# Normalising by feature tile: the input rows are turned once, the conditioning weights come in wider rows

## The chip, the cores and the metric

One core of a Trainium2 chip runs one launch of the kernel. The metric is the device time of that launch in microseconds. Engines are called by their functions: TensorE (PE; its weight loads are PEld), VectorE (DVE), ScalarE (ACT), GpSimd (POOL), and SyncE (SP), whose queue issues nearly all the DMAs.

## The reference

One inference step of a decoder layer for 1024 prompt tokens and 8 x 4 sample tokens, width 1024, all in float32. The first lines are those that matter here:

```python
mod = jax.nn.silu(c) @ w_ada + b_ada                      # one row per sequence (9 of them), 6 * 1024 columns
sh1, sc1, g1, sh2, sc2, g2 = split(mod, 6)
h = rmsnorm(x, norm_mix_w) * (1.0 + sc1) + sh1            # x * rsqrt(mean(x*x) + EPS) * w
z = h @ w_in + b_in                                       # 8 slices of 1024 columns
```

z feeds an HGRN2 recurrence with 8 heads of 128 and a gated depthwise convolution over 31 tokens; the two are gated, joined, multiplied by w_out and added to x; then come a second norm, a SwiGLU feed-forward part of width 2816 and a last norm. The six outputs are y for both groups and both groups' recurrent and convolution states.

## The kernel before

**Layout.** Everything is kept turned: features on the 128 partitions, the 1056 tokens (1024 prompt, 32 sample) along the free axis, 8 feature tiles (NJ). A float32 product is made of three: each operand is split in a high part and a low part (the rest), and hi*hi, hi*lo and lo*hi are summed. So for each block of weights (128 columns, 512 KB) ScalarE makes w_hi, VectorE or GpSimd makes w_lo = w_raw - w_hi (the helper low), and TensorE multiplies them with h_hi and h_lo in three groups of 352 tokens.

**The head of the program,** which the change rewrites, runs once before all of that. SP's queue (from L504) loads the conditioning vectors, four tiles of 128 tokens of x in four row buffers, 13 small loads of vectors, the conditioning weights of feature tile 0 (load_mod, L516: shift and scale, 512 KB each, in rows of 128 columns, that is 512 bytes), the other five tiles of x as the row buffers come free, the first two blocks of w_in, and the conditioning weights of tiles 1 to 7, for which there are three buffers (WADA). Each load into a used buffer waits for its readers.

For each tile t of tokens, ScalarE squares the row with a running sum (L1836), GpSimd makes the root's reciprocal rs9 (L2130, L2132), VectorE multiplies the row by it into xn (L1263). TensorE turns both x and xn, 8 transposes of 128x128 each, into PSUM (turn, L790). ScalarE copies x out of PSUM to xt (L1829), which is kept for the residual; VectorE copies the normed one to xh (L1256). In between VectorE and ScalarE do the small work on the lower bounds (lower_bounds, L1242). ScalarE and GpSimd split the two first blocks of w_in (L1813, L2107).

Then, for each feature tile j, TensorE makes the conditioning products in four groups of 32 rows (conditioning, L814: 32 products), ScalarE copies them out (acols, L1849), TensorE sums the groups (fold_groups, L827), and VectorE adds the bias (L1276), makes am = (1 + sc1) * w (L1283), then the modulated tile twice over: ScalarE writes its high part h_hi (L1851 for the prompt, L1853 for the samples) and VectorE the whole in float32 (L1287, with L1290 and L1292 for the 32 sample tokens), from which it takes h_hi to get h_lo (L1294). As soon as a feature tile is there, first_tiles (L835) multiplies it with both of the first two blocks of w_in: 9 matmuls for a block, 18 for a feature tile. Conditioning for tile kt + 2 goes ahead of tile kt's products, and its fold between the two blocks:

```python
for kt in range(NJ):
    if kt + 2 < NJ:
        conditioning(kt + 2)
    ...
    pe.wait_ge(h_ready, kt + 1)
    for b in range(2):
        ... 9 matmuls ...
        if b == 0 and kt + 2 < NJ:
            fold_groups(kt + 2)
```

After the last feature tile, the first block's PSUM banks are read, and the steady part begins: z_tile (L894) for each head, the convolution taps and the recurrence on VectorE beside it, and later the merge and the feed-forward products. It is the same in both kernels. SP issues there in program order: w_in blocks 2 and 3, the old convolution rows, then the store of xt (4.2 MB in two DMAs) which the residual reads much later.

Every wait is a semaphore written out by hand. The order of one engine is its program order; Steps.settle makes an engine wait for its own last instruction. GpSimd starts making masks (L2144) after the last h_ready.

## Time and profile before

| | |
|---|---|
| median of 3 runs | 1974.66 us (1973.8 to 1977.93) |
| the profiled execution's own time | 1975.14 us |
| its span in the profile | 1973.4 us |
| mean granted TensorE clock | 0.994 |
| TensorE busy | 1935.4 us, 16182 matmuls |
| VectorE, ScalarE, GpSimd busy | 1316.6, 655.9, 232.5 us |
| DMA | 237.45 MB, mean 120 GB/s |

A row of the view by line names the line, engine, operation, tiles, shapes and count, then busy time and mean ns of one, then the idle time before them. A row of the timeline or of the chain begins with start and duration in us. A busy engine overlaps its own instructions at the ends, so the distance between the starts of two that follow each other is a little less than a duration. TensorE's clock is given as a share of 2.4 GHz; 0.50 is its lower level of 1.2 GHz.

### The profile page before, as it was taken

What the parts mean: (1) busy time and instruction counts of PE and PEld (TensorE: products, weight loads), DVE (VectorE), ACT (ScalarE), POOL (GpSimd) and SP (SyncE); (2) the same over time, 40 slices, a digit from 0 to 9 for tenths busy, and PEclk for the clock granted to TensorE, in tenths of its full rate; (3) what the DMA queues carried; (4) which work ended last, traced back from release to release, by engine and by line L of the source; (5) the groups of instructions that cost most, each with busy time, mean ns of one, the idle gap of its engine ahead of it and who ended that gap; (6) DMA issues with size and microseconds to landing.
All of it is one profiled execution on the core that took longest, in us unless ns stands there. A gap on an engine that the chain in (4) does not pass through costs nothing.

```text
span 1973.4 us, 39636 instructions
## 1 busy us (share of the span) xinstructions
PE 1935.4 (98%) x16182; PEld 1876.1 (95%) x16182; DVE 1316.6 (67%) x1800; ACT 655.9 (33%) x1066; POOL 232.5 (12%) x256
## 2 busy tenths in 40 slices
PE   7999999999999999998999999999999999999998
PEld 6999999999999999988989999999999999999998
DVE  6697979786878788897775665554445544465543
ACT  6212313131413222233544433333343333433332
POOL 2300000000000000021132554700000000000000
PEclk8999999999999999999999999999999999999999
DMA  8723041413232222222366644444444544444443
GB/s 254 229 61 87 24 112 45 112 45 92 66 90 67 70 77 79 78 75 93 107 216 210 187 135 139 132 138 140 136 137 143 154 136 136 135 147 148 138 133 110
DMA packets 417245, 237.45 MB, mean 120 GB/s; under 512 B 16375, under 2 KB 411287, under 8 KB 417072
## 3 DMA queue, kind: packets, MB, share of 16 engines
q1 hardware_dynamic: 416672, 234.48, 40.6%
q8 instruction: 118, 1.93, 0.4%
q10 hardware_dynamic: 416, 0.72, 0.1%
q14 instruction: 39, 0.32, 0.0%
HBM read 211.91 MB, written 24.11 MB: 120 GB/s over the span
## 4 chain that ended last, share of the span: by engine, by line
PE 83%; DVE 10%; ACT 3%; issue 2%; DMA 1%; DVEq 0%; POOL 0%; ACTq 0%; SPq 0%
PE Z L887 45%; PE Z L905 27%; DVE yb L1453 4%; DVE w_lo L1305 2%; PE R L980 1%; PE Z L852 1%; PE R L924 1%; ACT w_hi L1813 1%; PE R L1006 1%; PE R L930 1%; PE R L1013 1%; PE R L1015 1%; PE R L987 1%; DVE S L1420 1%; DMA w_raw<-in_w_out_dram 1%
## 5 line engine op out<-in xcount | busy, mean ns | idle before, releaser
L1813 ACT ACTIVATE w_hi<-w_raw 128x1024 fp32r<-128x1024 f32 (+1 forms) x316 | 329.4, 1043 | 932.3 <-PE Z L887 469.7
L1305 DVE TENSOR_TENSOR w_lo<-w_raw,w_hi 128x1024 fp32r<-128x1024 f32 (+1 forms) x305 | 386.0, 1266 | 369.1 <-ACT w_hi L1813 361.4
L905 PE MATMUL Z<-h_hi,w_hi 128*128 128x352 f32 x1488 | 499.7, 336 | 2.8 <-issue 1.7
L905 PE MATMUL Z<-h_hi,w_lo 128*128 128x352 f32 x1488 | 478.4, 321 | 0.0
L905 PE MATMUL Z<-h_lo,w_hi 128*128 128x352 f32 x1488 | 477.8, 321 | 0.0
L1453 DVE SCALAR_TENSOR_TENSOR yb<-up,vec,yb 128x1024 f32 (+1 forms) x240 | 327.2, 1363 | 28.8 <-DVE yb L1453 3.7
L887 PE MATMUL Z<-h_hi,w_hi 128*128 128x352 f32 x1056 | 342.1, 324 | 0.0
L887 PE MATMUL Z<-h_hi,w_lo 128*128 128x352 f32 x1056 | 339.2, 321 | 0.0
L887 PE MATMUL Z<-h_lo,w_hi 128*128 128x352 f32 x1056 | 338.6, 321 | 0.0
L905 PEld LDWEIGHTS Z<-h_hi,w_hi 128*128 128x128 f32 x1488 | 279.5, 188 | 20.2 <-issue 16.7
L905 PEld LDWEIGHTS Z<-h_lo,w_hi 128*128 128x128 f32 x1488 | 280.3, 188 | 0.5 <-issue 0.5
L905 PEld LDWEIGHTS Z<-h_hi,w_lo 128*128 128x128 f32 x1488 | 279.3, 188 | 0.0
L887 PEld LDWEIGHTS Z<-h_lo,w_hi 128*128 128x128 f32 x1056 | 198.7, 188 | 0.0
L887 PEld LDWEIGHTS Z<-h_hi,w_lo 128*128 128x128 f32 x1056 | 198.4, 188 | 0.0
L887 PEld LDWEIGHTS Z<-h_hi,w_hi 128*128 128x128 f32 x1056 | 198.1, 188 | 0.0
L887 PE MATMUL Z<-act_hi,w_hi 128*128 128x352 f32 x528 | 170.8, 323 | 0.0
L887 PE MATMUL Z<-act_hi,w_lo 128*128 128x352 f32 x528 | 169.6, 321 | 0.0
L887 PE MATMUL Z<-act_lo,w_hi 128*128 128x352 f32 x528 | 169.3, 321 | 0.0
L887 PEld LDWEIGHTS Z<-act_hi,w_lo 128*128 128x128 f32 x528 | 99.4, 188 | 0.0
L887 PEld LDWEIGHTS Z<-act_lo,w_hi 128*128 128x128 f32 x528 | 99.2, 188 | 0.0
L887 PEld LDWEIGHTS Z<-act_hi,w_hi 128*128 128x128 f32 x528 | 99.1, 188 | 0.0
L2190 POOL TENSOR_TENSOR gate<-ta,tb 128x1056 f32<-128x1056 f32 x8 | 21.2, 2645 | 626.0 <-DVE O L1439 480.8
(303 smaller groups left out, 2408.8 us busy)
## 6 DMA issues: line engine op xcount, KB each, us to landing
w_raw<-in_w_ffn_in_dram SPq DMA_DIRECT2D x132, 512.0 KB, 3.8
w_raw<-in_w_in_dram SPq DMA_DIRECT2D x64, 512.0 KB, 5.0
w_raw<-in_w_out_dram SPq DMA_DIRECT2D x48, 512.0 KB, 4.2
w_raw<-in_w_ffn_out_dram SPq DMA_DIRECT2D x48, 512.0 KB, 4.0
aw<-in_w_ada_dram SPq DMA_DIRECT2D x32, 512.0 KB, 4.0
w_raw<-in_w_ffn_out_dram SPq DMA_DIRECT2D x24, 384.0 KB, 3.4
ada_w<-in_w_ada_dram SPq DMA_DIRECT2D x16, 512.0 KB, 6.2
mbuf<-merged_scratch SPq DMA_DIRECT2D x32, 176.0 KB, 4.3
```

Of the source, the lines that this page charges most:

```text
L852: last = mm(Z[b][:, g, 0:GW], w[:, kt, :], x[:, kt, g * GW:(g + 1) * GW], start=kt == 0 and m == 0, stop=kt == NJ - 1 and m == 2)
L887: last = mm(out, w[:, kt, :], x(kt, g), start=first and kt == 0 and m == 0, stop=last_block and kt == n - 1 and m == 2)
L905: last = mm(out, w[:, kt, :], x[:, kt, cols], start=kt == 0 and m == 0, stop=kt == NJ - 1 and m == 2)
L924: return transpose(out, in_, ident[0:m, 0:m])
L930: last = mm(bank[group:group + 32, ADA_COL:ADA_COL + P], ct[:, kt, :], aw[:, kt, :], start=kt < 4, stop=kt >= 4)
L980: last = mm(bank[p:p + BAND, c * w:(c + 1) * w], k[:, t:t + BAND], halves(qd[:, t:t + BAND], 1 << lv, 1), start=True, stop=True)
L987: last = mm(bank[p:p + b, c * b:(c + 1) * b], k[:, t:t + b], qd[:, t + b:t + 2 * b], start=True, stop=True)
L1006: last = mm(bank[:, c * P:(c + 1) * P], ktok[:, cc, :], vtok[:, cc, :], start=True, stop=True)
L1305: st.tell(V.tensor_tensor(w_lo[b.par][:, 0:n, :], w_raw[b.par][:, 0:n, :], w_hi[b.par][:, 0:n, :].bitcast(F32), ALU.subtract), w_split, b. ...
L1453: ins = V.scalar_tensor_tensor(yp, xp, w, yp, ALU.mult, ALU.add)
L1813: A(w_hi[b.par][:, 0:n, :], w_raw[b.par][:, 0:n, :], ACT.Copy).then_inc(w_hi_ready, 1)
L2190: st.tell(Q.tensor_tensor(gate[:, :], ta[:, :], tb[:, :], ALU.mult), gate_ready, h.v)
```

## The change

The normed rows xn and their turning are gone. x alone is turned, and VectorE copies it out of PSUM, where ScalarE did. The reciprocal roots, one per token, are spread over all partitions by nine small products (root_row: rs9's column times the identity) and copied to rsrow, a row of 1056 per partition. For each feature tile VectorE multiplies xt by am and by rsrow in one operation with two SBUF inputs (scale_prompt), ScalarE adds the shift as it writes h_hi, and VectorE adds the shift and takes h_hi away in a second such operation (prompt_low). In VectorE's order the scaling of tile j stands ahead of the low part of tile j - 1. The 32 sample tokens move to GpSimd (samples: four small operations for each feature tile) with a semaphore of their own, hs_ready. The fold goes after the second of the three product groups of the first block. The lower bounds move in among the feature tiles.

All nine tiles of x have buffers of their own, in the memory of h_hi and h_lo, so no load of x waits. The conditioning weights come for two feature tiles at a time, in rows of 256 columns (1 KB): four pairs of 2 x 1 MB, two buffers. The first pair goes behind all of x; the third waits for conditioning 1, the fourth for conditioning 3. On GpSimd the first samples stand between the low parts of the two first blocks. The diff, cut:

```diff
-XN = 8
-WADA = 3
+WADA = 2
-XBUF = 4
...
-    xn, xh = at("xn", [P, XN, D], F32, A1), at("xh", [P, NJ, T], F32, A2)
+    xrow = at("xrow", [P, NC + 1, D], F32, A1)
...
+    ada_w = [e(f"ada_w{i}", [P, 2, 8, 2 * P]) for i in range(WADA)]
+    rsrow = e("rsrow", [P, T])
+    xs, hs = e("xs", [P, NJ, TS]), e("hs", [P, NJ, TS])
...
             def load_x(t):
-                if t >= XBUF:
-                    sp.wait_ge(x_squared, t - XBUF + 1)
-                    sp.wait_ge(xn_scaled, t - XBUF + 1)
-                    sp.wait_ge(x_turned, 2 * (t - XBUF + 1))
...
+            def load_mod(pair):
+                if pair >= WADA:
+                    sp.wait_ge(ada_done, 2 * (pair - WADA + 1))
                 for sec in (SH1, SC1):
+                    col = sec * D + 2 * pair * P
+                    sp.dma_start(ada_w[pair % WADA][:, sec, :, :], wada_v[:, :, col:col + 2 * P]) \
+                        .then_inc(adaw_loaded[pair % WADA], 16)
...
-            load_mod(0)
-            for t in range(XBUF, NC + 1):
+            for t in range(4, NC + 1):
                 load_x(t)
...
+            load_mod(0)
             for b in range(2):
                 load_first(b)
-            for j in range(1, NJ):
-                load_mod(j)
+            for pair in range(1, NJ // 2):
+                load_mod(pair)
...
+            def root_row(t):
+                m = tokens(t)
+                pe.wait_ge(rms_ready, t + 1)
+                wait(pe, row_copied, t - 2)
+                mm(row_bank(t), rs9[0:m, t:t + 1].to_broadcast([m, P]), ident[0:m, 0:m], start=True, stop=True) \
+                    .then_inc(row_made, 1)
...
             for t in range(NC + 1):
-                pe.wait_ge(x_loaded[t % XBUF], 16 * (t // XBUF + 1))
-                turn(t, xrow[t % XBUF], 0, x_turned, x_evac)
-                if t:
-                    turn_normed(t - 1)
+                turn_tokens(t)
+                if t >= 2:
+                    root_row(t - 2)
...
                     pe.wait_ge(h_ready, kt + 1)
+                    pe.wait_ge(hs_ready, kt + 1)
                     for b in range(2):
                         for m, (w, x) in enumerate(((w_hi[b], h_hi), (w_hi[b], h_lo), (w_lo[b], h_hi))):
...
+                            if b == 0 and m == 1 and kt + 2 < NJ:
+                                fold_groups(kt + 2)
...
-                        if b == 0 and kt + 2 < NJ:
-                            fold_groups(kt + 2)
...
-                st.do(V.tensor_scalar(buf[:, 0:TP], xh[:, j, 0:TP], am[:, j, 0:1], mod[:, SH1 * NJ + j, 0:1],
-                                      ALU.mult, ALU.add))
...
+            def scale_prompt(j):
                 st.settle()
+                st.tell(V.scalar_tensor_tensor(hbuf[j % 3][:, 0:TP], xt[:, j, 0:TP], am[:, j, 0:1], rsrow[:, 0:TP],
+                                               ALU.mult, ALU.mult), h_full, j + 1)
+            def prompt_low(j):
                 dve.wait_ge(h_hi_ready, j + 1)
+                st.tell(V.scalar_tensor_tensor(h_lo[:, j, 0:TP], hbuf[j % 3][:, 0:TP], mod[:, SH1 * NJ + j, 0:1],
+                                               h_hi[:, j, 0:TP].bitcast(F32), ALU.add, ALU.subtract), h_ready, j + 1)
+
+            condition(0)
+            condition(1)
+            scale_prompt(0)
+            for j in range(1, NJ + 1):
+                if 1 < j < NJ:
+                    condition(j)
+                if j < NJ:
+                    scale_prompt(j)
+                prompt_low(j - 1)
+                if j == 2:
+                    lower_bounds_in()
+                if j == 5:
+                    lower_bounds()
+            dve.wait_ge(hs_ready, NJ)
...
+            for j in range(2):
+                groups_out(j)
+                hi(Idx(j))
+            for j in range(NJ):
+                act.wait_ge(h_full, j + 1)
+                A(h_hi[:, j, 0:TP], hbuf[j % 3][:, 0:TP], ACT.Identity, bias=mod[:, SH1 * NJ + j, 0:1]) \
+                    .then_inc(h_hi_ready, 1)
+                if 0 < j < NJ - 1:
+                    groups_out(j + 1)
...
-            for b in range(2):
-                low(Idx(b))
+            pool.wait_ge(row_copied, NC + 1)
+            pool.wait_ge(x_evac, N_TURNS)
+            st.tell(Q.tensor_tensor(xs[:, :, :], xt[:, :, TP:T], rsrow[:, TP:T].unsqueeze(1).to_broadcast([P, NJ, TS]),
+                                    ALU.mult), xs_scaled, 1)
+            low(Idx(0))
+            def samples(j):
+                pool.wait_ge(am_ready, j + 1)
...
+                st.do(Q.tensor_tensor(seqs(xs[:, j, :]), seqs(xs[:, j, :]), per_seq(am[:, j, 1:NSEQ]), ALU.mult))
+                st.settle()
+                st.do(Q.tensor_tensor(seqs(h_hi[:, j, TP:T]), seqs(xs[:, j, :]), shift, ALU.add))
+                st.do(Q.tensor_tensor(seqs(full), seqs(xs[:, j, :]), shift, ALU.add))
+                st.settle()
+                st.tell(Q.tensor_tensor(h_lo[:, j, TP:T], full, h_hi[:, j, TP:T].bitcast(F32), ALU.subtract),
+                        hs_ready, j + 1)
+            samples(0)
+            low(Idx(1))
+            for j in range(1, NJ):
+                samples(j)
```

## Rows read from the trace of the kernel before

**Rows 1.** The page, part 1: busy us, share of the span, instructions.

```profile
PE 1935.4 (98%) x16182; PEld 1876.1 (95%) x16182; DVE 1316.6 (67%) x1800; ACT 655.9 (33%) x1066; POOL 232.5 (12%) x256
```

**Rows 2.** Stretches: us, busy of each engine (instructions), TensorE's clock, DMA share, GB/s.

```profile
0.00:31.50 31.50, 22.36 (x156) 20.49 (x156) 19.54 (x34) 23.89 (x43) 9.95 (x34) 0.95 0.87 264
31.50:40.70 9.20, 5.55 (x105) 4.52 (x105) 8.49 (x18) 3.13 (x5) 3.69 (x2) 0.73 1.02 271
...
35.80:42.60 6.80, 4.75 (x43) 4.24 (x44) 5.66 (x12) 3.35 (x6) 0.00 (x0) 0.50 0.96 251
```

**Rows 3.** The chain that ended last, 0 to 76 us: start, duration, what.

```profile
1.21 1.87 DMA crow<-in_c_sample_dram
...
38.87 1.87 PE R L823 x32
40.74 2.49 PE Z L852 x9
...
66.39 5.91 PE Z L852 x36
...
74.71 0.14 issue
```

**Rows 4.** TensorE's timeline, one feature tile.

```profile
45.05 1.08 PE L823 MATMUL R<-ada_w,ct 128*32 128x128 f32 x32
46.06 0.76 PE L852 MATMUL Z<-h_hi,w_hi 128*128 128x352 f32 x3
...
47.14 0.65 PE L852 MATMUL Z<-h_hi,w_lo 128*128 128x352 f32 x3
47.63 0.51 PE L831 MATMUL R<-fold,acols 128*128 128x9 f32 x4
...
49.62 1.08 PE L823 MATMUL R<-ada_w,ct 128*32 128x128 f32 x32
```

**Rows 5.** The view by line, each shape apart, of the first 75 us.

```profile
L1256 DVE COPY xh<-Z 128x512 f32<-128x512 f32 x16 | 10.5, 687 | 3.3 <-PE Z L797 3.2
```

**Rows 6.** Timelines of VectorE and of GpSimd, 30 to 36 us.

```profile
31.41 1.49 DVE L1244 TENSOR_TENSOR lbs<-lbs 128x8 f32<-128x8 f32 x1
...
33.17 2.04 DVE L1248 TENSOR_TENSOR lbs<-lbs 128x8 f32<-128x8 f32 x1
...
30.52 4.67 POOL L2107 TENSOR_TENSOR w_lo<-w_raw,w_hi 128x1024 fp32r<-128x1024 f32 x2 [1.42 <-ACT w_hi L1813]
```

**Rows 7.** Stretches as above, by what the DMAs moved in them.

```profile
0.00:10.00 10.00, 4.37 (x24) 4.38 (x25) 2.95 (x4) 6.68 (x10) 3.57 (x19) 1.00 0.67 234
...
4.00:8.00 4.00, 2.37 (x15) 2.38 (x16) 2.15 (x3) 2.76 (x6) 1.03 (x3) 1.00 0.98 363
...
24.00:32.00 8.00, 6.75 (x71) 5.62 (x73) 7.53 (x14) 7.39 (x16) 3.68 (x7) 1.00 1.19 298
...
64.00:70.00 6.00, 6.00 (x52) 5.80 (x42) 4.31 (x9) 3.21 (x5) 0.00 (x1) 1.00 1.03 411
```

**Rows 8.** Timelines of VectorE (two stretches) and of ScalarE.

```profile
48.17 0.36 DVE L1276 TENSOR_SCALAR mod<-R,vec 128x9 f32<-128x9 f32 x2 [1.14 <-PE R L831]
...
48.90 0.81 DVE L1287 TENSOR_SCALAR ta<-xh,am,mod 128x1024 f32<-128x1024 f32 x1
...
50.33 1.26 DVE L1294 TENSOR_TENSOR h_lo<-ta,h_hi 128x1056 fp32r<-128x1056 f32 x1 [0.30 <-ACT h_hi L1853]
...
88.97 1.28 DVE L1453 SCALAR_TENSOR_TENSOR yb<-up,vec,yb 128x1024 f32<-128x1024 f32 x1
90.17 1.22 DVE L1305 TENSOR_TENSOR w_lo<-w_raw,w_hi 128x1024 fp32r<-128x1024 f32 x1
...
32.73 0.39 ACT L1849 ACTIVATE acols<-R 128x256 f32<-128x256 f32 x1 [1.34 <-PE R L823]
```

**Rows 9.** The 32-token GpSimd operation of the second norm: ns min/median/max.

```profile
L2280 POOL TENSOR_TENSOR h2buf<-h2buf,mod x8: 241/243/402, 1244.3 to 1281.7; 128x32 f32<-128x32 f32 x8
```

**Rows 10.** A stretch as above, after the middle of the run.

```profile
1001.60:1008.50 6.90, 6.61 (x23) 5.80 (x22) 6.90 (x13) 2.05 (x3) 1.56 (x2) 0.51 0.46 157
```

More of the change, by code:

```diff
@@ L324, in program @@
     ht = e("ht", [P, NJ, NS * HIST])
-    ada_w = [e(f"ada_w{i}", [P, 2, 8, P]) for i in range(WADA)]
-    xrow = [e(f"xrow{i}", [P, D]) for i in range(XBUF)]
+    ada_w = [e(f"ada_w{i}", [P, 2, 8, 2 * P]) for i in range(WADA)]
     vrow = e("vrow", [P, 4, P])
+    rsrow = e("rsrow", [P, T])
+    xs, hs = e("xs", [P, NJ, TS]), e("hs", [P, NJ, TS])
     hbuf = (ta, tb, ysum)
@@ L788, in vectors, with turn_tokens @@
                 last.then_inc(p0_done, 1)
-            def turn(t, row, normed, done, read):
+            def turn_tokens(t):
+                pe.wait_ge(x_loaded[t], 16)
                 m = tokens(t)
                 for n in range(2 * t, 2 * t + 2):
-                    wait(pe, read, n - 2)
-                    bank = turn_bank(normed, n)
+                    wait(pe, x_evac, n - 2)
+                    bank = turn_bank(n)
                     for j in range(4):
-                        last = transpose(bank[:, j * m:(j + 1) * m], row[0:m, (4 * (n % 2) + j) * P:(4 * (n % 2) + j + 1) * P],
-                                         ident[0:m, 0:m])
-                    last.then_inc(done, 1)
-            def turn_normed(t):
-                pe.wait_ge(xn_scaled, t + 1)
-                turn(t, xn[:, t % XN, :], 1, xn_turned, xn_evac)
+                        c = (4 * (n % 2) + j) * P
+                        last = transpose(bank[:, j * m:(j + 1) * m], xrow[0:m, t, c:c + P], ident[0:m, 0:m])
+                    last.then_inc(x_turned, 1)
+            def root_row(t):
[4 more added lines that the diff above has]
+                    .then_inc(row_made, 1)
             for t in range(NC + 1):
-                pe.wait_ge(x_loaded[t % XBUF], 16 * (t // XBUF + 1))
-                turn(t, xrow[t % XBUF], 0, x_turned, x_evac)
-                if t:
-                    turn_normed(t - 1)
+                turn_tokens(t)
+                if t >= 2:
+                    root_row(t - 2)
                 if t == 2:
                     vectors()
-            turn_normed(NC)
+            for t in range(NC - 1, NC + 1):
+                root_row(t)
             def conditioning(j):
-                pe.wait_ge(adaw_loaded[j % WADA], 32 * (j // WADA + 1))
+                pair, c = j // 2, j % 2 * P
+                pe.wait_ge(adaw_loaded[pair % WADA], 32 * (pair // WADA + 1))
                 if j < 2:
@@ L823, in conditioning @@
                         last = mm(R[j % 2][group:group + 32, sec * P:(sec + 1) * P], ct[:, kt, :],
-                                  ada_w[j % WADA][:, sec, kt, :], start=kt < 4, stop=kt >= 4)
+                                  ada_w[pair % WADA][:, sec, kt, c:c + P], start=kt < 4, stop=kt >= 4)
                 last.then_inc(ada_done, 1)
@@ L1842, in _ @@
                     A(lbs[:, 1, :], lbs[:, 1, :], ACT.Exp).then_inc(lb_exp, 1)
-            turned_evac(NC)
-            for b in range(2):
-                hi(Idx(b))
-            for j in range(NJ):
-                act.wait_ge(ada_done, j + 1)
-                A(acols[:, j % 2, :, :].rearrange("p s n -> p (s n)"), R[j % 2][:, 0:2 * P], ACT.Copy).then_inc(acols_ready, 1)
-                act.wait_ge(am_ready, j + 1)
-                A(h_hi[:, j, 0:TP], xh[:, j, 0:TP], ACT.Identity, bias=mod[:, SH1 * NJ + j, 0:1], scale=am[:, j, 0:1])
-                act.wait_ge(h_full, j + 1)
-                A(h_hi[:, j, TP:T], hbuf[j % 3][:, TP:T], ACT.Copy).then_inc(h_hi_ready, 1)
             A(ms9[:, 0:1], eps[:, :], ACT.Sigmoid)
@@ L2133, in _ @@
                         rms_ready, t + 1)
-            for b in range(2):
-                low(Idx(b))
+            pool.wait_ge(row_copied, NC + 1)
[5 more added lines that the diff above has]
+                pool.wait_ge(am_ready, j + 1)
+                if j == 0:
+                    pool.wait_ge(xs_scaled, 1)
+                full, shift = hs[:, j, :], per_seq(mod[:, SH1 * NJ + j, 1:NSEQ])
+                st.do(Q.tensor_tensor(seqs(xs[:, j, :]), seqs(xs[:, j, :]), per_seq(am[:, j, 1:NSEQ]), ALU.mult))
[9 more added lines that the diff above has]
+                samples(j)
             pool.wait_ge(h_ready, NJ)
```

76 lines of the change are left out of this document (28 added, 48 removed).

## The prediction, made before the changed kernel ran

> **What bounds the kernel now.** I read the page first: TensorE is busy 1935 us of a span of 1973 us [rows 1]. Nothing in the change touches the heads, the merge or the feed-forward part, so all it can do is move the moment from which TensorE hardly stops again. The view of stretches finds it: the first 31.5 us hold 22.4 us of matmuls, the next 9.2 us only 5.6 [rows 2]. After that the chain stays on TensorE until the first block is done.
>
> The chain of the first 75 us gives the two marks of the head [rows 3]: the first product of the first feature tile starts at 40.74, and the first block's last product ends at 66.39 + 5.91 = 72.3. Behind it a block is split on ScalarE and VectorE and the steady part begins, 0.14 us after VectorE ends. All that stays, so the quantity to forecast is by how much 72.3 moves.
>
> **The head, as it is.** Between 40.7 and 72.3 TensorE is the bound: one feature tile costs 4.57 us, from conditioning at 45.05 to the next at 49.62 [rows 4]: 1.01 for 32 conditioning products, 3.56 for the two blocks with the fold between them. VectorE needs 3.42 us of the 4.57 (48.17 to 51.59 [rows 8]), and has its low part ready long before it is wanted.
>
> **What the change removes.** (1) The second turning: 72 TensorE transposes, nine scalings and 18 copies on VectorE, of 0.69 us at full size [rows 5]. In their place VectorE makes the 18 copies of x that ScalarE made, and nine row copies of a quarter of that width. 18 x 0.69, one more for the vectors and nine of a third of that, 0.23, make 15.2 us at most. TensorE turned its first tiles within the first 10 us [rows 7], so from about 8 they end near 23. They end at 31.4 now, where the lower bounds begin [rows 6]. (2) The lower bounds leave the road to the first tile. They took from 31.41 to 35.4 there, since two additions and products of eight columns lasted 1.49 and 2.04 us and both ended as a GpSimd w_lo did: two of those fill 30.52 to 35.19, 2.35 us each, and the ends are 32.90 and 35.21 [rows 6]. That is worth some 3 us at that place, but the head start meets other limits first.
>
> **The weights' arrival becomes the first of them.** The first 10 us moved 2.34 MB [rows 7], which is the first four tiles of x and the vectors. The other 2.23 MB of x are now issued at about 8.4, where the first conditioning load stood, without waiting for buffers: at the 363 GB/s that x had [rows 7], they are through at 16.1. Behind them comes the first pair, 2.10 MB in rows of 1 KB. No row has such rows; 512-byte rows moved at 298 GB/s and 4-KB rows at 411 [rows 7]. I take 350, the middle: 6.0 us, to 22.1. From the last byte to the semaphore I allow 1.0 us (between nothing and the 1.87 us for which the chain waits for the first load, 32 KB in all [rows 3]). So conditioning can begin at 23.1. The two blocks of w_in (1.05 MB at 298) follow until 25.6, the second pair until 31.6, and it is signalled at 32.6. Conditioning of tile 2 stands in TensorE's queue ahead of the first product and needs that pair. TensorE idles before it, as it did before the stretch of 0.50 clock [rows 2], where the same 32 products took 1.87 instead of 1.01 [rows 3, 4]: the first product can't start before 34.5.
>
> **The port is the second.** Conditioning 0 at 23.1, 1.01; evacuation 0.39 and 0.04 to start the next; fold 0.54 (47.63 to 48.17); conditioning 1 until 26.1; evacuation and fold until 27.1; VectorE's bias and scale 0.73 (48.17 to the scaling at 48.90), to 27.8 [rows 4, 8]. Meanwhile the first block (landed at 24.9) has its high part made on ScalarE by 25.9 (a 1024-column pass is about 1 us on it), and GpSimd's w_lo runs from 25.9 to 28.3. The new prompt operations have two SBUF inputs like the ones that stalled at 31.41, so I let them exclude GpSimd's. From 28.3, in any order: three VectorE operations of 1.28 us (two scalings and the first low part, priced by the 1.28 us of the tap product of the same shape [rows 8]), four sample operations of 0.24 [rows 9] and the second w_lo, 2.35: 7.15 us, to 35.45, and 0.14 from VectorE's end to TensorE's start [rows 3]. The first product starts at 35.6: 5.1 us earlier than 40.74.
>
> Whether VectorE also keeps GpSimd out, these rows do not isolate. The Trainium skill's page "SBUF — State Buffer" (SBUF: two separate sides) says that it does: whichever starts first has the shared ports for its whole instruction. Without that, GpSimd's small operations would cost nothing here and the first product would start 1.0 us earlier.
>
> **Then the head start is eaten.** This is the step I weigh most. The new order on VectorE is bias and scale of tile j, scaling of tile j, low part of tile j-1. The next product tile needs that low part, and it now stands behind a fold that is made in the tile before. One round: six products 1.08 (46.06 to 47.14 [rows 4]), the fold to VectorE's start 0.54, bias and scale 0.73, the scaling 1.20 (pitch of such operations back to back [rows 8]), the low part 1.28, 0.14 to TensorE: 4.97 us against TensorE's own 4.57. The old code made the same low part without another 1.28 us operation ahead of it. ScalarE's evacuation is ready about 0.7 us before the fold wants it. Six rounds, then the last three half tiles: 5.91 us for four halves now [rows 3], so 4.4. From 35.6: 29.8 + 4.4 = 69.8. A first tile at half clock adds 1.0 (its first block took 2.49 us [rows 3] where a later one took 1.57 [rows 4], 0.92). A GpSimd sample operation between VectorE's two adds 0 to 0.24 each round; I take 0.1, in all 0.6. Sum: 71.4 against 72.3, 0.9 us earlier.
>
> **Costed at nothing.** The nine root products (TensorE would wait for 23.1 anyway; if the weights came earlier, the last root, near 20.6, would show). The third load of a pair waits for conditioning 1, near 26, long before the queue reaches it; the fourth for conditioning 3, about 4.6 us after the first product, so at 40.2; it lands by 48.5, and is wanted four rounds after the first product, at 55: 6 us of cover. SP's w_in blocks, the old convolution rows and the x store stand behind it, and are not wanted before 72. ScalarE's wait for the lower bounds falls into its idle time.
>
> **Against the times.** The profiled execution took 1975.1 us for its span of 1973.4; the median is 1974.7. Taking off 0.9 gives 1974.2 and 1973.8: I forecast 1973.8 for the median. A measurement tells 0.2%, 3.9 us, from no change.
>
> **Rivals.**
> - *Faster.* The pair lands early and the clock is up: conditioning 2 ends near 33.7; VectorE and GpSimd slip past each other, first product at 33.9; the round is 4.8, between TensorE's 4.57 and my 4.97. 33.9 + 28.8 + 4.4 = 67.1, 5.2 us earlier, 1969.5. For it: 411 GB/s was seen, and TensorE worked at full clock just before its long wait [rows 2]. Against it: no row lets the low part come sooner. 26%.
> - *The wide rows bring nothing.* At 298 GB/s the first pair is signalled at 24.1 and the second at 34.7; conditioning 2 ends at 36.6, the first product starts at 36.7, the end is 72.5, 1974.9. In this the change does not do what its second half says. Also within 0.2%. For it: 298 was a steady rate with the engines always busy. Against it: the 4-KB rate is higher, so length counts. 14%.
> - *Slower.* GpSimd's four sample operations, released by the same signal as VectorE's scaling, all fall into VectorE's chain: 4 x 0.24 makes the round 5.93 instead of 5.07, six times 0.86 is 5.2 us, the end 76.6, 4.3 later, 1979.0. It decides from a round of 5.8 us. For it: the stalls at 31.41 and 33.17. Against it: only one GpSimd operation can be waiting at a time, and two of the four follow on another's end. 14%.
>
> The Trainium skill speaks for the second: "DMA: Bandwidth & Descriptors" (Specifications) puts full rate at 512 bytes and more, so doubling a 512-byte row would be worth nothing. This trace disagrees in part (298 against 411 GB/s), but between different kinds of transfer.
>
> **How the numbers follow.** The forecast has 46%, and lies within 0.2% with the second rival: same 60%, faster 26%, slower 14%. The range reaches to the faster rival's 1969.5; upward it takes the late weights (1.1 us), one more for a whole tile at half clock and a round of 5.3 (1.4 us): 1977.3, short of the slower rival. One thing outside the head can move: a stretch of half clock at 1001.6 to 1008.5 [rows 10], where 6.9 us of products lose about 3. It follows a stretch in which TensorE waited, and may fall elsewhere.
>
> **What would show it.** Right: no DVE wait of 1.5 and 2 us ahead of the first conditioning; first product near 35.6; rounds of about 5.0 with TensorE waiting for the low part's line; first steady product near 74. Wrong: rounds of 4.6 (then the gain is the head start's whole 4 to 5 us), or of 5.8; a fourth pair that TensorE waits for; DMA under 300 GB/s between 16 and 32 us.

## The result, and the profile after

The changed kernel takes 1980.7 us in the median of nine runs (1979.3 to 1982.9), the kernel before 1976.8 us in nine (1973.8 to 1977.9): a ratio of 1.0022, interval 1.0014 to 1.0030. It is slower by 4 us where a gain of 0.9 was forecast, and the time lies above the range. The forecast of 1973.8 set out from 1974.7, the median of three runs; the nine give 1976.8, so 2.1 us of its distance to 1980.7 lie in the starting point. The profiled execution took 1981.2 us for a span of 1979.4; the span before was 1973.4. So 6.0 us are to be found in this pair of traces, and some 4 in the medians.

The page, part 1, of the changed kernel, which answers to [rows 1]:

```profile
PE 1934.9 (98%) x16128; PEld 1872.7 (95%) x16128; DVE 1314.7 (66%) x1784; ACT 645.6 (33%) x1040; POOL 253.1 (13%) x289
```

TensorE is as busy as it was. The 6 us are waiting, so they have to be found as waits. The chain of the first 80 us, with the same columns as [rows 3]:

```profile
24.27 9.62 DMA ada_w<-in_w_ada_dram
33.93 1.93 PE R L829 x32
35.87 2.10 issue
37.97 2.10 PE Z L859 x6
...
45.23 1.16 PE Z L859 x6
...
51.72 0.38 DVE mod L1279 x2
52.12 0.30 DVE am L1286
52.45 1.37 DVE tb L1291
53.82 1.21 DVE h_lo L1297
55.07 1.24 PE Z L859 x6
...
69.96 4.62 PE Z L859 x27
74.66 1.07 ACT w_hi L1828
```

The first product of a tile starts at 37.97 (40.74 before, 35.6 forecast). The first block ends at 69.96 + 4.62 = 74.6 (72.3 before, 71.4 forecast). The head start of 2.8 us at the first product has turned into a delay of 2.3 us. From 50.10 on the rounds are exactly the forecast's: VectorE's four operations stand in the chain, the product that ends one round starts at 55.07, and the round is 4.97 us long (products of a new tile start at 50.10, 55.07, 60.04, 65.00 and 69.96). What is not as forecast lies before 45. TensorE's timeline there:

```profile
24.61 1.93 PE L829 MATMUL R<-ada_w,ct 128*32 128x128 f32 x32 [2.96 <-DMA ada_w<-in_w_ada_dram]
...
27.99 1.94 PE L829 MATMUL R<-ada_w,ct 128*32 128x128 f32 x32
```

and the stretches, with the columns of [rows 2]:

```profile
23.30:43.80 20.50, 13.61 (x125) 11.99 (x126) 11.48 (x14) 6.13 (x8) 10.43 (x13) 0.50 0.83 250
27.00:33.00 6.00, 3.91 (x40) 3.24 (x40) 3.72 (x6) 2.26 (x3) 4.73 (x6) 0.50 1.10 346
```

All three conditionings before the first product last 1.93 us instead of 1.01, and the granted clock is 0.50, its level of 1.2 GHz, from 23.3 to 43.8, which takes in the whole first tile. TensorE's turning, with the root products, ends at 21.7; then it waits 2.96 us for the weights and soon 2.48 for the next pair. Before, it went on turning to 31.0, waited 0.6 us and made the first conditioning at full clock, and the half clock ahead of the first product lasted 6.8 us, from 35.8.

The chain writes 2.10 us down to "issue" before the first product, where TensorE waits for several semaphores. VectorE's and GpSimd's timelines give the real releaser:

```profile
28.01 2.35 POOL L2117 TENSOR_TENSOR w_lo<-w_raw,w_hi 128x1024 fp32r<-128x1024 f32 x1 [5.32 <-ACT w_hi L1828]
28.50 1.89 DVE L1286 TENSOR_SCALAR am<-mod,ones,vec 128x9 f32<-128x9 f32 x1
31.52 2.34 POOL L2117 TENSOR_TENSOR w_lo<-w_raw,w_hi 128x1024 fp32r<-128x1024 f32 x1
31.89 1.99 DVE L1286 TENSOR_SCALAR am<-mod,ones,vec 128x9 f32<-128x9 f32 x1
33.92 1.37 DVE L1291 SCALAR_TENSOR_TENSOR ta<-xt,am,rsrow 128x1024 f32<-128x1024 f32 x1
34.28 1.10 POOL L2158 TENSOR_TENSOR h_hi<-xs,mod 128x32 fp32r<-128x32 f32 x1
35.32 1.35 DVE L1291 SCALAR_TENSOR_TENSOR tb<-xt,am,rsrow 128x1024 f32<-128x1024 f32 x1
36.59 1.27 DVE L1297 SCALAR_TENSOR_TENSOR h_lo<-ta,mod,h_hi 128x1024 fp32r<-128x1024 f32 x1
```

VectorE's am, nine columns, ends with GpSimd's second w_lo, at 33.88 and 33.86; then three operations follow without a gap, and the low part ends at 37.86, 0.11 before the product. It is the chain behind the shared port that releases the first product, as forecast, only later.

The other part of the time is behind the head. From ScalarE's w_hi (74.66, before 72.37) to the end of the span 1904.7 us pass, before 1901.0: 3.7 us in a stretch in which no instruction was changed. Those are two single executions; the median less the mark gives 1906.0 and 1904.4, 1.6 us. TensorE's waits, with releaser, us in total, times, longest. The changed kernel:

```profile
PE Z L894 <- DVE m_lo_a L1586: 4.5, 4, 2.3
PE R L977 <- DVE q0s L1329: 4.2, 6, 0.9
PE Z L894 <- DVE w_lo L1320: 1.6, 4, 0.7
```

and the kernel before, the same three:

```profile
PE Z L887 <- DVE m_lo_a L1571: 3.8, 5, 1.9
PE R L970 <- DVE q0s L1314: 3.5, 5, 0.8
PE Z L887 <- DVE w_lo L1305: 0.9, 3, 0.4
```

Three waits for the same operations of VectorE have grown by 0.7 us each, 2.1 of the 3.7, in code that is the same in both kernels.

### The profile page after: what moved, and what is told of

It reads as the page before. It is cut to its first block, busy times and chain, and to the rows that moved or that the text cites. A ratio compares the mean times of both kernels' runs of the same rounds, so it can differ in the third digit from the quotient of the medians.

```text
span 1979.4 us, 39513 instructions
## 1 busy us (share of the span) xinstructions
PE 1934.9 (98%) x16128; PEld 1872.7 (95%) x16128; DVE 1314.7 (66%) x1784; ACT 645.6 (33%) x1040; POOL 253.1 (13%) x289
## 4 chain that ended last, share of the span: by engine, by line
PE 79%; DVE 13%; issue 3%; ACT 3%; DMA 1%; SPq 1%; DVEq 0%; ACTq 0%; POOL 0%
PE Z L894 44%; PE Z L912 25%; DVE yb L1468 4%; DVE w_lo L1320 2%; PE R L987 1%; ACT w_hi L1828 1%; PE R L931 1%; PE Z L859 1%; PE R L1013 1%; PE R L1020 1%; PE R L937 1%; DVE S L1435 1%; PE R L1022 1%; PE R L994 1%; DMA w_raw<-in_w_out_dram 1%
```

## The experiments

From here on "w_hi" is the start of ScalarE's first split after the first block, the mark of the head's end, and "behind" is the span less that mark.

**1. The low part ahead of the next fold's work** (VectorE no longer makes tile j's low part behind the scaling of tile j + 1):

```diff
-            for j in range(1, NJ + 1):
-                if 1 < j < NJ:
-                    condition(j)
-                if j < NJ:
-                    scale_prompt(j)
-                prompt_low(j - 1)
+            scale_prompt(1)
+            prompt_low(0)
+            prompt_low(1)
+            for j in range(2, NJ):
+                condition(j)
+                scale_prompt(j)
+                prompt_low(j)
```

> The changed kernel, but on VectorE the low part of tile j stands ahead of the wait for fold j + 1, not behind it. Theory (order): rounds of 4.97 us come from the low part standing behind the fold of the tile before; now the rounds fall to TensorE's own 4.57 and the 1.34 us wait ahead of the seventh tile goes. First product of the first tile unchanged near 38.0, the first block ends near 71.7 instead of 74.6, 2.9 us off the whole. Rival (port): GpSimd's sample operations set the round; it stays at 4.97 and the end near 74.6. Rival (clock): the loss is all in the half-clock stretch of 23 to 44 us; same end as the changed kernel.

Ratio to before 1.0013 (1.0004 to 1.0023), median 1978.6. Its chain:

```profile
46.99 1.38 DVE ta L1291
...
48.39 1.16 ACT h_hi L1857
...
49.57 1.29 DVE h_lo L1297
```

VectorE's operations of one tile now pass ScalarE's h_hi in between, and the round is 4.57 (the next tile's h_lo starts at 54.14). The first product is at 37.85 and w_hi at 71.7, 3.0 us before the changed kernel's. So the order on VectorE was worth 3 us of the head: some 0.4 in each of the rounds, and the wait of 1.34 ahead of the seventh tile, where TensorE has no conditioning to make. 1905.4 us follow behind. The median is 2.1 us under the changed kernel's.

**2. TensorE kept busy while it waits** (idle products of the identity: 26 before the first conditioning, 22 after the second, 18 after the third):

```diff
+            def keep_busy(n):
+                for _ in range(n):
+                    mm(Z[0][:, 0, 0:P], ident[:, :], ident[:, :], start=True, stop=True)
...
+                keep_busy(26)
                 for j in range(2):
                     conditioning(j)
                     fold_groups(j)
+                keep_busy(22)
...
                         conditioning(kt + 2)
+                    if kt == 0:
+                        keep_busy(18)
```

> The changed kernel with 66 idle 128x128 products on TensorE, whose result nothing reads: 26 before the first conditioning, 22 after the second fold, 18 after the third conditioning, about as long as TensorE sits idle there. Theory (clock): the granted clock does not fall to half between 23 and 44 us, the 32 conditioning products take 1.0 instead of 1.93 us, the first product starts near 35.6 (the second pair of weights still lands at 33.9), the first round is 4.97 instead of 7.2, the first block ends near 70.0, 4.6 us off the whole. Rival (weights and port): the head waits for the weights and for VectorE and GpSimd anyway, the start stays within 1 us of 38.0 and the gain is under 2.5 us, from the first round alone. Rival: idle products do not hold the clock; no change, or 1 us slower where they outlast the wait.

The idle products were twice as long as I took them to be, 0.23 us each, so that they themselves became the bound: the first product came at 43.9, w_hi at 78.3, the ratio was 1.0040 (1.0025 to 1.0054). As a test of the time it failed. What the filler does to the clock can still be read in its stretches:

```profile
22.10:25.50 3.40, 3.40 (x17) 3.40 (x18) 0.00 (x0) 0.00 (x0) 0.57 (x1) 0.50 1.21 303
25.50:44.00 18.50, 17.50 (x222) 16.50 (x222) 9.24 (x9) 5.22 (x7) 9.27 (x10) 1.00 0.73 233
```

With TensorE at work the half clock is over at 25.5 instead of 43.8. It still fell at 22.1, though the filler began only 0.33 us after the last root product: the filler shortened the half clock and did not prevent it. At 1.00 the first round takes 4.93 us (43.89 to 48.82), where the changed kernel's takes 7.26, so the half clock costs 2.3 us in that round.

**3. The pairs fetched in 512-byte rows** (the same bytes in twice as many loads, everything else as in the changed kernel):

```diff
-                    col = sec * D + 2 * pair * P
-                    sp.dma_start(ada_w[pair % WADA][:, sec, :, :], wada_v[:, :, col:col + 2 * P]) \
+                    for c in range(2):
+                        col = sec * D + (2 * pair + c) * P
+                        sp.dma_start(ada_w[pair % WADA][:, sec, :, c * P:(c + 1) * P], wada_v[:, :, col:col + P]) \
...
```

> The changed kernel, with each pair's weights fetched as four DMAs in rows of 128 columns (512 bytes) instead of two in rows of 256. Same bytes, same order, same buffers. Theory (row length counts): 512-byte rows move at about 298 GB/s and 1-KB rows at 349, so the second pair's conditioning starts near 36 instead of 33.9, and the whole is 1.5 to 2 us slower than the changed kernel. Rival (row length brings nothing, or the extra time is covered by VectorE's chain): within 0.5 us of the changed kernel.

```profile
27.00:33.00 6.00, 4.51 (x52) 3.38 (x44) 2.68 (x6) 2.66 (x4) 3.68 (x6) 0.50 1.18 293
```

In the same six microseconds 293 GB/s instead of 346. The third conditioning starts at 36.37 instead of 33.93, but the first product only 1.05 us later (39.02) and w_hi 1.3 us later (76.0). The first conditioning came 1.05 us later too (25.66), and the chain behind the port passed on that and no more. The ratio is 1.0027 (1.0017 to 1.0036): from the changed kernel's not told apart. The wide rows do what the change says, and are worth 1 us of the head.

**4. Both first w_lo on VectorE** (1.22 us each there, where GpSimd takes 2.35 and holds VectorE back meanwhile):

```diff
+            def first_low(b):
+                dve.wait_ge(w_hi_ready, b + 1)
+                st.tell(V.tensor_tensor(w_lo[b][:, :, :], w_raw[b][:, :, :], w_hi[b][:, :, :].bitcast(F32), ALU.subtract),
+                        w_split, b + 1)
...
             condition(0)
+            first_low(0)
             condition(1)
+            first_low(1)
             scale_prompt(0)
...
-            low(Idx(0))
...
-            low(Idx(1))
```

> The changed kernel with both first w_lo made on VectorE (1.2 us each) instead of GpSimd (2.35 each). Theory (port): the two am operations that last 1.89 and 1.99 us beside GpSimd's w_lo fall back to 0.29, saving 3.3 us on VectorE for 2.4 us added; the first product starts near 37.3 instead of 38.0, and the whole is 0.7 us faster than the changed kernel. Rival (no port): the am operations stay long, and VectorE's 2.4 us are added to the start: 40.3 and 2 us slower.

```profile
33.15 0.29 DVE L1286 TENSOR_SCALAR am<-mod,ones,vec 128x9 f32<-128x9 f32 x1
33.35 1.22 DVE L1302 TENSOR_TENSOR w_lo<-w_raw,w_hi 128x1024 fp32r<-128x1024 f32 x1
33.52 1.15 POOL L2161 TENSOR_TENSOR xs<-xs,am 128x32 f32<-128x32 f32 x1 [1.40 <-DVE am L1286]
```

am takes 0.29 us again, and now it is GpSimd's 32-token operation that lasts 1.15 us, the length of VectorE's w_lo, instead of 0.24: exclusion in both directions. From conditioning 1 to the end of the low part 0.65 us were saved. But in this run the first weights landed 1.25 us later, and the head ended later all the same (first product 38.57, w_hi 75.4). Ratio 1.0015 (1.0006 to 1.0025).

**5. The changed kernel with the short filler alone** (10 idle products before the first conditioning, 18 after the second, none after the third):

```diff
+                keep_busy(10)
                 for j in range(2):
                     conditioning(j)
                     fold_groups(j)
+                keep_busy(18)
```

> The changed kernel with 28 idle products alone (10 before the first conditioning, 18 between the second and the third), so that TensorE comes out of the half clock as early as in the kernel with all three edits. Theory (the half clock that lasts through the first tile is what the prediction missed in the head): half clock for some 3.4 us only, the third conditioning at 34 in 1.08 us instead of 1.93, the first product near 36.5 to 37, first round 5.0 to 5.4 instead of 7.3 us, rounds of 4.97 as before, first block's end near 71.5 to 72.5, that is 2 to 3 us earlier than in the changed kernel; the time 1976 to 1980, according to the place of the program. Rival (VectorE's chain holds the head, the clock is hidden behind it): first product and first block's end within 0.7 us of the changed kernel's, 37.3 to 38 and 74 to 75.

```profile
35.41 2.28 issue
37.70 1.20 PE Z L865 x6
...
43.82 1.17 PE Z L865 x6
```

Between the two theories. The third conditioning is done 0.46 us earlier, at 35.41, and yet the first product comes only 0.27 us earlier: there the rival was right, VectorE's chain releases it. The first round takes 6.12 us instead of 7.26, and w_hi is at 73.3, 1.4 us earlier. That is what this filler gained, not the price of the half clock, since two things worked against it. Its 10 products ran at half clock for the most part (0.51 from 22.3 to 25.7) and took 4.10 us, so that the first conditioning started at 25.96, 1.35 us later than without them. And VectorE's second scaling fell beside GpSimd's second w_lo (32.95 to 35.32), after which the clock halved once more:

```profile
32.92 3.48 DVE L1297 SCALAR_TENSOR_TENSOR tb<-xt,am,rsrow 128x1024 f32<-128x1024 f32 x1
```

```profile
39.00:42.80 3.80, 3.80 (x19) 3.42 (x22) 3.38 (x7) 1.15 (x1) 2.60 (x4) 0.55 0.01 2
```

The median is 1979.1, 1.6 us under the changed kernel's (ratio to before 1.0010, 1.0001 to 1.0019), about as much as the head gained; the two kernels' intervals overlap.

**6. All three together**: the order of 1, the w_lo of 4, the short filler of 5. VectorE's part:

```diff
             condition(0)
+            first_low(0)
             condition(1)
+            first_low(1)
             scale_prompt(0)
...
+            scale_prompt(1)
+            prompt_low(0)
+            prompt_low(1)
```

> The changed kernel with the three repairs: the low part ahead of the next fold, both first w_lo on VectorE, and 28 idle products on TensorE in two of its waits (10 ahead of the first conditioning, 18 ahead of the third), this time no longer than the waits. Theory (order, clock and port account for the head): the clock stays up, conditioning of the third tile at 33.9 to 34.9, first product near 35.1, rounds of 4.57, the first block ends near 66 us, 6 us before that of the kernel before and 8.5 before that of the changed one. Of the whole I expect 3 us less than before (1973), since the changed kernel also lost some 2 to 3 us behind the head; 6 us less (1970) if that loss goes with the head's. Rival (weights): the second pair lands later than 34.5 and the first block ends after 68.

Ratio 0.9980 (0.9971 to 0.9989), median 1972.5: by 0.2% faster than the kernel before, clear of noise. First product at 36.2, w_hi at 68.1, 4.3 us ahead of the kernel before and 6.6 of the changed one; the median is 4.3 and 8.2 us lower. The head is 2 us later than expected, in part since this filler too outlasts the wait (first conditioning at 26.05). The end of its head:

```profile
61.33 4.92 PE Z L865 x30
...
68.11 1.07 ACT w_hi L1842
```

**7. What lies behind the head.** With the head's 2.3 us told, 1.6 us of the medians (3.7 in the profiled pair) were open. One theory was that the later head shifts the loop over the heads against its loads. So the kernel before was made late on purpose, with 12 idle products before the last tile:

```diff
+                    if kt == 7:
+                        for _ in range(12):
+                            mm(R[0][:, 0:P], ident[:, :], ident[:, :], start=True, stop=True)
```

> The kernel before, with 12 idle 128x128 products on TensorE between conditioning and the products of the last feature tile; at 0.23 us each (as the idle products of the earlier run were at full clock) the head is 2.8 us longer and nothing else changes. Theory (the head passes through): the whole is 2.8 us slower than before and the time from the end of the first block to the last product is that of before, 1890.6 us within 0.5. Rival (the steady part depends on when it starts): that stretch grows or shrinks by more than 1.5 us, so that the whole differs from before by under 1.3 or over 4.3 us.

w_hi comes at 74.7, 2.3 us later as in the changed kernel, but the time is 1991.8, ratio 1.0082 (1.0067 to 1.0096): 15 us more, of which the head explains 2.3. (Its profiled execution is the fastest of five, 1987.8.) TensorE's waits show a kind that was nearly absent:

```profile
PE Z L908 <- issue: 10.2, 7, 3.0
```

"Issue" is time in which TensorE waits for nothing that the profile shows. The 12 products moved the loop in time, and, being 48 instructions by the page's count, also on in TensorE's program. The next kernels move it in the program and not in time.

**8 and 9. Padding in idle time**, in the kernel before and in the changed one:

```diff
             pe.wait_ge(const_ready, 2)
+            for _ in range(20):
+                transpose(Z[0][:, 0, 0:P], ident[:, :], ident[:, :])
...
+            for n in range(8):
+                V.memset(attc[:, 0, n:n + 1], 0.0)
...
+            for n in range(8):
+                Q.memset(h2buf[:, n:n + 1], 0.0)
```

> The kernel before with instructions that do nothing in times when the engines idle anyway: 20 transposes on TensorE in its first wait, 8 memsets of one column on VectorE and 8 on GpSimd. All later instructions stand at other places in the engines' programs; the head must end at 72.3 as before. Theory (places in the program matter): the stretch behind the head moves by 1 us or more from 1890.6, and the whole with it. Rival (they don't): stretch and whole as before within 0.5 us and 1 us.

> The changed kernel with the same idle instructions in the same idle times. Theory (places in the program matter): the stretch from the end of the first block to the last product, 1894.4 us in the changed kernel against 1890.6 before, moves by 1 us or more, and the steps of 0.25 us in every second head move too. Rival (they don't): 1894.4 within 1 us, the whole as the changed kernel's.

The kernel before, padded: 1993.8, ratio 1.0083 (1.0069 to 1.0096), although its head ends earlier, w_hi at 70.9. The changed one, padded: 1980.1, 1.0018 (1.0009 to 1.0027), no difference that can be told from the unpadded one. The waits of the first, and its timeline around the longest:

```profile
PE Z L907 <- issue: 12.8, 6, 4.0
PE R L972 <- DVE q0s L1318: 6.5, 4, 4.1
```

```profile
446.65 0.32 PE L907 MATMUL Z<-h_hi,w_lo 128*128 128x352 f32 x1
...
450.96 0.66 PE L907 MATMUL Z<-h_hi,w_hi 128*128 128x352 f32 x1 [3.99 <-issue]
```

The kernel before has a gap at the same product, shorter:

```profile
447.69 0.42 PE L905 MATMUL Z<-h_hi,w_hi 128*128 128x352 f32 x1 [1.02 <-issue]
```

The DMA part for 440 to 452 us of the padded kernel before (queue, kind, packets, MB, share) says what moves there:

```profile
q8 instruction: 3, 0.05, 1.8%
```

The program itself is fetched, in packets of 16 KB. By the trace's packets one of the three starts at 448.14, inside the gap, and takes 1.46 us, to 449.6; TensorE goes on at 450.96. The gap comes again, 3.94 us long, ahead of the product at 667.74, 216.8 us on, and not in the pass between; there too such a packet moves inside it. That TensorE waits for its own program there is the reading that fits; no row names the packet as the releaser.

**10 and 11. Which engine's place?** The kernel before with the 20 transposes of the last diff alone, and with its 16 memsets alone:

> The kernel before with 20 idle transposes (40 of TensorE's instructions, some 3 us) in TensorE's idle time at the start, and nothing else. Theory (the place of TensorE's own instructions decides: its instructions arrive in blocks, and where the loop over the heads lies in the blocks sets whether it runs dry): the head ends where it did or earlier (72.4 or less), and the waits of the heads' loop marked as issue grow as with all the padding, from 1.7 to some 12 us, gaps of 4 us near 446 and 663; the time 1990 to 1995. Rival (VectorE's place decides): gaps of 1.3 us at most, 1975 to 1978. Rival 2 (both): 1980 to 1988.

> The kernel before with 8 tiny memsets more on VectorE and 8 on GpSimd at the start, TensorE's program untouched. Theory (TensorE's place decides): the time of the kernel before, 1975 to 1979, issue waits of TensorE some 1.7 us. Rival (VectorE's place): 1985 to 1994, with VectorE arriving late at q0s in the heads.

Transposes alone: 1989.8, ratio 1.0073 (1.0059 to 1.0087), 11.6 us of issue waits in the heads, two of them of 4.2 and 4.0 us. Memsets alone: 1982.0, ratio 1.0030 (1.0018 to 1.0042), 1.3 us of issue waits, but TensorE waits 7.8 us for q0s instead of 3.5. The first theory holds for the issue waits: they come with TensorE's padding alone. The memsets' loss is of another kind. 4.2 us of it are one wait of TensorE, and ahead of it VectorE and GpSimd do this:

```profile
880.03 3.28 DVE L1313 TENSOR_TENSOR qd<-q,f 128x1056 f32<-128x1056 f32 x1 [0.37 <-DVE yb L1455]
882.98 2.53 POOL L2109 TENSOR_TENSOR w_lo<-w_raw,w_hi 128x1024 fp32r<-128x1024 f32 x1 [0.79 <-ACT w_hi L1815]
883.24 2.31 DVE L1314 COPY k0s<-k 128x32 f32<-128x32 f32 x1
```

The copy of 32 columns takes 2.31 us and ends with GpSimd's w_lo, at 885.55 and 885.51, like am in the head. In the kernel before the same copy has run before that w_lo starts (882.25):

```profile
881.12 0.17 DVE L1312 COPY k0s<-k 128x32 f32<-128x32 f32 x1
```

So the shared port explains this part, once the two meet; the kernel with both paddings has the same 2.31 us at 896.43, and the one with the transposes alone has 0.17. Why the memsets let them meet no row says, and that VectorE waits for its own program is not shown. By the medians the one padding costs 14.1 us and the other 6.3 (before had 1975.7 beside them), and both together 17.0 (before had 1976.8 there).

**12. The fastest kernel, padded** with the 20 transposes alone:

```diff
             pe.wait_ge(const_ready, 2)
+            for _ in range(20):
+                transpose(Z[0][:, 0, 0:P], ident[:, :], ident[:, :])
```

> The fastest kernel so far (the change with the low parts ahead of the next fold, both first low weights on VectorE, 28 idle products between the conditionings) with 20 idle transposes more at TensorE's start, which cost nothing there. It asks how much of that kernel's gain is its program's place. Theory (the head's gain of 4.2 us is real, the place adds or takes some us of its own): the head ends at 68 to 69 as without them; the time 1970 to 1992 according to the heads' issue waits, and the time less those waits within 2 us of the unpadded kernel's time less its own. Rival (the head's gain is lost with the place): the head ends at 72 or later.

1985.7, ratio 1.0050 (1.0036 to 1.0064). The head keeps 2.7 of its 4.3 us (w_hi at 69.7; the third conditioning started at 35.24 instead of 34.49), and 10.5 us of issue waits in the heads take them back. Less its issue waits the median is 5.0 us above the unpadded kernel's less its own, where 2 at most were expected, so the issue waits are not the whole of what the padding costs. All but the last column are from the profiled executions, whose own times stand beside the medians:

| kernel | w_hi | behind | TensorE's issue waits in the heads | its time, us | median, us |
|---|---|---|---|---|---|
| before | 72.4 | 1901.0 | 1.7 | 1975.1 | 1976.8 |
| before, memsets | 72.3 | 1908.4 | 1.3 | 1982.4 | 1982.0 |
| before, 12 products | 74.7 | 1911.3 | 10.2 | 1987.8 | 1991.8 |
| before, transposes | 72.3 | 1915.8 | 11.6 | 1989.8 | 1989.8 |
| before, both paddings | 70.9 | 1922.6 | 12.8 | 1995.3 | 1993.8 |
| changed | 74.7 | 1904.7 | 1.5 | 1981.2 | 1980.7 |
| changed, both paddings | 73.9 | 1902.8 | 1.5 | 1978.7 | 1980.1 |
| changed, low part first | 71.7 | 1905.4 | 1.8 | 1978.9 | 1978.6 |
| changed, long filler | 78.3 | 1905.6 | 1.2 | 1985.7 | 1984.1 |
| changed, 512-byte rows | 76.0 | 1903.2 | 1.4 | 1980.9 | 1981.3 |
| changed, w_lo on VectorE | 75.4 | 1903.7 | 1.9 | 1980.8 | 1979.6 |
| changed, short filler | 73.3 | 1904.8 | 2.2 | 1979.9 | 1979.1 |
| changed, all three | 68.1 | 1901.7 | 2.3 | 1971.6 | 1972.5 |
| changed, all three, transposes | 69.7 | 1911.3 | 10.5 | 1982.7 | 1985.7 |

No instruction behind w_hi differs in work between these kernels, and the stretch takes between 1901.0 and 1922.6 us. The fastest and the slowest execution of one kernel lie 2 to 9 us apart, so differences of 2 us in this column say little. The median less w_hi is steadier: 1904.4 for the kernel before, 1906.0 for the changed one, 1906.2 for the changed one padded, and 1904.4 for the fastest. The padded changed kernel's 1902.8 is from the fastest of its eleven runs.

## Why the prediction was wrong

Right in its mechanisms and in most of the marks of the head:
- **What the change removes**: the turning ended at 21.7 (forecast near 23), the lower bounds left the road.
- **The round** of 4.97 us came out, and its terms stand in the chain. That it is exact to 0.01 us is luck: the six products took 1.23 (forecast 1.08) and the scaling 1.37 (1.20), the fold 0.39 (0.54), the low part 1.20 (1.28) and the step to TensorE 0.05 (0.14), and the errors cancel. Undone (experiment 1), the round is 4.57 and the head 3.0 us shorter.
- **The port** does exclude both engines, and the chain behind it released the first product. The sentence of the Trainium skill's page "SBUF — State Buffer" (SBUF: two separate sides) that whichever starts first has the shared ports for its whole instruction agrees with the traces: am 1.89 and 1.99 us beside w_lo, 0.29 without; GpSimd's 32 tokens 1.10 to 1.24 beside VectorE's scaling, 0.24 without.
- **The fourth pair, the root products and the w_in blocks behind the pairs** cost nothing, as said: TensorE waits for weights twice only, before tiles 0 and 2. The first two w_in blocks did cost something (below).
- **The slower rival's mechanism** (GpSimd's sample operations in VectorE's chain) did not happen. In the rounds GpSimd waits for VectorE, not the other way: in the chain VectorE's operations follow each other within 0.04 us. The time came out on that rival's side by other causes.
- **"The wide rows bring nothing"** fell with experiment 3: 346 GB/s, where 350 was taken, against 293. So did the page "DMA: Bandwidth & Descriptors" (Specifications) of the Trainium skill for this transfer, by whose rule 512-byte rows run at full rate already.

Two steps failed.

**"The weights' arrival" and the times built on it.** It put the first conditioning at 23.1; it came at 24.61, 1.5 us later. The forecast let x, the pair and the two w_in blocks arrive one after the other, at 363, 350 and 298 GB/s. x did as forecast (359 GB/s from 10 to 16 us), and the pair had its rate too, but late:

```profile
15.00:18.00 3.00, 2.43 (x21) 1.95 (x19) 3.00 (x7) 1.71 (x5) 1.34 (x5) 1.00 1.07 254
18.00:22.00 4.00, 3.39 (x27) 2.58 (x25) 3.87 (x12) 2.23 (x4) 1.74 (x6) 1.00 1.10 345
```

Where x ends and the pair begins, 254 GB/s moved; that holds back some 0.3 MB, 0.9 us (an estimate, at 350 GB/s). And the first w_in block did not wait for the pair: by the trace's packets its 512-byte rows move from 22.12 us, and 589 of them, 0.30 MB and another 0.9 us, are through before the pair's last row lands at 23.78 (22.1 forecast). So the rates were right, and "one after the other" was wrong. Why the rate is low where x ends stays open.

**The half clock** was the other part of that step. The forecast gave it to the conditioning of tile 2 and, as 1.0 us, to the first tile's first block. But the clock was at 0.50 from 23.3 to 43.8, over all three conditionings and the whole first tile. The work that was removed had kept TensorE busy to 31.0, and now it has none from 21.7 to 24.6. The clock fell with the fillers of experiments 2, 5 and 6 too, so this wait is not shown to be why it fell. What the missing work cost is the return: 2.4 GHz was back at 25.5 with the filler of experiment 2, and at 43.8 without it.

Added up: the weights 1.5 us late and the first conditioning 0.9 longer, less 0.4 (in the forecast the high part waited for w_in until 24.9, when the first conditioning had been copied out at 24.5), put ScalarE's first w_hi at 26.88 and GpSimd's first w_lo at 28.01 (25.9), 2.1 us late. From the end of that w_lo to the end of the low part it took 7.50 us instead of 7.15, since GpSimd's four sample operations fill 1.16 us and not 0.96, and VectorE's three 3.94 and not 3.84. So the first product is 2.4 us late. From it to the next tile's 45.23 it took 7.3 us, where the forecast allowed 6.1; the five rounds to 69.96 took 0.6 less than allowed, since the 0.1 for GpSimd's operations was not needed, and the last half tiles 0.2 more: 71.4 + 2.4 + 1.2 - 0.6 + 0.2 = 74.6. Of the clock's share, 0.9 in the first conditioning and 2.3 in the first round (experiment 2), the forecast had 1.0. No run separates the late weights from the clock: the fillers of experiments 2, 5 and 6 put the first conditioning later still.

**"Nothing in the change touches the heads", and so "all that stays".** The instructions stay, their places in the engines' programs do not: the change takes 123 instructions out of the program (39,636 and 39,513 on the pages), all of them ahead of the loop over the heads. Experiments 8 and 10 to 12 show that instructions which cost nothing where they stand add 6 to 17 us to the whole, of the kernel before and of the fastest; to the changed kernel (9) they add nothing that can be measured. So the 3.7 us behind the changed kernel's head (1.6 in the medians) are less than places can make, and their cause stays open: the changed kernel has no more issue waits than the one before (1.5 and 1.7 us), and what grew are waits for VectorE. The granted clock is 0.57 between 914 and 918 us in the changed kernel, one more dip than before had; but the fastest kernel has the like between 906 and 910, and the changed kernel with the low part first has none and still takes 1905.4 behind, so the dip doesn't explain it.

A shift of the stretch of half clock near 1001 [rows 10], which I had named as the one thing outside the head, did not matter: it is at 1003.0, as long as before.

## What to carry to other kernels

Work that is removed ahead of a wait leaves TensorE idle, so ask of every stretch taken out what it kept at full clock, and price the products behind the wait at 1.2 GHz too: here they took 7.26 us where 4.93 were possible. Where an engine's order changes, add up its operations from the signal that starts a round to the one that ends it and compare with TensorE's own round: that sum told 4.97 against 4.57 here. A difference of 0.2% between two versions is no verdict on an edit while a few idle instructions at the start of either move it by more: pad both, read the issue waits of the long loops, and judge the edit by its own stretch.

## What was not expected of the hardware

- 20 idle transposes in TensorE's free time at the start cost 14 us at the end (ratio 1.0073, 1.0059 to 1.0087). TensorE's issue waits in the heads grew from 1.7 to 11.6 us, in gaps of up to 4.2 us, and a packet of the instruction queue moves in each of the two longest. 16 memsets of one column on VectorE and GpSimd cost 6 (1.0030, 1.0018 to 1.0042), of which one wait of 4.2 us is a copy of 32 columns on VectorE that met a w_lo on GpSimd.
- The port's exclusion is not a matter of width: an operation of nine columns whose other operands are single columns waited 1.6 and 1.7 us, and GpSimd's 32-column additions were drawn out fivefold.
- The gain of the wide rows, 346 against 293 GB/s, with the DMA engines as busy in both (shares of 1.10 and 1.18).
